# A hybrid decoder layer with 32 experts: x1 kept on chip, VectorE adds the ranks inside the last expert, and each next first weight quarter issued ahead of the down halves

## The reference

```
x1  = x + merge_branches(...)                  # residual, 520 rows
h   = rms_norm(x1, g_ffn)
logits = h @ w_router + b_router               # 32 experts
top_v, top_e = top_k(logits, 4); gates = softmax(top_v)
for each row and each of its 4 experts e:
    gu   = h @ w_gu[e] + b_gu[e]               # 1024 -> 2048
    gate = min(gu[:1024], 7); up = clip(gu[1024:], -7, 7)
    act  = (up + 1) * gate * sigmoid(1.702 * gate)
    y   += gates[e] * (act @ w_down[e] + b_down[e])
out = rms_norm(x1 + y, g_final)
```

## Time and profile before

| | |
|---|---|
| median of 3 runs | 1601.92 us (1600.48 to 1602.94) |
| the profiled execution's own time | 1602.56 us |
| its span, first to last instruction | 1600.6 us |
| mean granted TensorE clock | 0.982 |
| TensorE busy | 1542.3 us, 96% |
| VectorE busy | 797.2 us, 50% |
| ScalarE busy | 280.1 us, 18% |
| GpSimd busy | 211.1 us, 13% |
| moved by DMA | 514.10 MB, mean 321 GB/s |
| first gate/up matmul of the loop | at 537.77 us |
| last down matmul | ends at 1554.22 us |

### The profile page before, as it was taken

How to read it: one execution, slowest core, us unless ns; L and a number is a source line. 1 busy time by engine, 2 the same in 40 slices (tenths; PEclk the granted TensorE clock), 3 DMA queues, 4 the chain that set the end, 5 groups by cost and what they waited for, 6 DMA issues and landing times.

```text
span 1600.6 us, 32912 instructions
## 1 busy us (share of the span) xinstructions
PE 1542.3 (96%) x13183; PEld 711.9 (44%) x13183; DVE 797.2 (50%) x2035; ACT 280.1 (18%) x556; POOL 211.1 (13%) x278
## 2 busy tenths in 40 slices
PE   9999999999999899999999999999999999999982
PEld 7677487787745433333333333333333333333320
DVE  4349738605523553445444544544454445444538
ACT  2310020006211011112111111121112111211122
POOL 3634310015100000000000000000000000000015
PEclk9999999999999799999999999999999999999996
DMA  7455745713262599999999999999999999999984
GB/s 240 156 165 184 261 167 177 257 61 119 92 287 78 196 416 417 415 409 419 416 411 407 416 415 411 411 414 413 407 410 414 417 406 415 417 417 404 415 333 161
DMA packets 73820, 514.10 MB, mean 321 GB/s; under 512 B 13570, under 2 KB 14018, under 8 KB 48538
## 3 DMA queue, kind: packets, MB, share of 16 engines
q1 hardware_dynamic: 63378, 493.35, 77.3%
q0 software_dynamic: 10384, 20.01, 3.7%
HBM read 499.60 MB, written 22.37 MB: 326 GB/s over the span
## 4 chain that ended last, share of the span: by engine, by line
PE 70%; DMA 24%; DVE 2%; POOL 2%; issue 2%; ACT 1%; SPq 0%; DVEq 0%; POOLq 0%; ACTq 0%
PE PS L1322 34%; DMA weight_ring<-w_gu 22%; PE PS L938 16%; PE PS L1246 3%; PE PS L1328 3%; PE PS L989 2%; PE PS L1054 2%; PE PS L1334 2%; PE PS L1040 1%; PE PS L1104 1%; DMA region_x<-x_rows 1%; POOL region_x L716 1%; PE PS L1003 1%; POOL weight_ring L625 1%; PE PS L1279 1%
## 5 line engine op out<-in xcount | busy, mean ns | idle before, releaser
L1322 PE MATMUL PS<-weight_ring,region_experts 128*32 128x512 f32 x5376 | 597.6, 593 | 7.1 <-DMA weight_ring<-w_gu 5.9
L1322 PEld LDWEIGHTS PS<-weight_ring,region_experts 128*32 128x32 f32 x5376 | 169.9, 110 | 401.8 <-issue 365.3
L1740 DVE TENSOR_TENSOR region_experts<-PS,region_w 128x512 f32<-128x512 f32 x96 | 66.4, 692 | 464.2 <-PE PS L1322 464.2
L1328 PE MATMUL PS<-weight_ring,act_turned 128*32 128x512 f32 x2048 | 225.6, 592 | 0.0
L938 PE MATMUL PS<-region_x,region_w 128*128 128x260 f32 (+1 forms) x928 | 209.4, 385 | 1.0 <-DVE region_x L1545 1.0
L938 PEld LDWEIGHTS PS<-region_x,region_w 128*128 128x128 f32 x928 | 175.2, 190 | 33.1 <-issue 4.6
L1731 DVE STREAM_TRANSPOSE region_experts<-region_x 32x256 f32<-32x256 f32 x372 | 161.2, 433 | 4.7
L865 ACT ACTIVATE region_experts<-region_experts 128x256 f32<-128x256 f32 x96 | 40.0, 416 | 615.2 <-DVE region_experts L1742 615.2
L1328 PEld LDWEIGHTS PS<-weight_ring,act_turned 128*32 128x32 f32 x2048 | 66.5, 110 | 153.2 <-issue 153.2
L683 POOL DMA_INDIRECT y_k<-region_x,idx_y x31 | 29.0, 934 | 680.4 <-ACT region_x L889 658.5
L1334 PE MATMUL PS<-weight_ring,act_turned 128*32 128x256 f32 x2048 | 116.4, 379 | 0.0
(11 more groups left out here) (282 smaller groups left out, 1153.9 us busy)
## 6 DMA issues: line engine op xcount, KB each, us to landing
weight_ring<-w_gu SPq DMA_DIRECT2D x112, 2048.0 KB, 12.4
weight_ring<-w_down SPq DMA_DIRECT2D x64, 2048.0 KB, 13.7
ring_more<-w_gu SPq DMA_DIRECT2D x16, 2048.0 KB, 21.6
region_w<-w_mt SPq DMA_DIRECT2D x33, 512.0 KB, 4.2
weight_ring<-cache_kT SPq DMA_DIRECT2D x64, 256.0 KB, 4.1
weight_ring<-cache_v SPq DMA_DIRECT2D x64, 256.0 KB, 4.0
weight_ring<-w_out SPq DMA_DIRECT2D x2, 2048.0 KB, 9.9
weight_ring<-y_k SPq DMA_DIRECT2D x2, 2048.0 KB, 16.1
```

The lines of the kernel that those rows point to most:

```text
L1322: mm = pe.matmul(bank(g)[GRP * q:GRP * q + GRP], hTe[u][:, k, GRP * g:GRP * g + GRP], weights(k // 2, u)[:, k % 2, SEG * q:SEG * q + SEG], ...
L1328: mm = pe.matmul(bank(3)[GRP * j:GRP * j + GRP], actT[:, kk, GRP * g:GRP * g + GRP], w_dn[:, kk, 512 * h:512 * h + 512], start=(kk == 0), ...
L1740: dve.tensor_tensor(gu, bank(g), b_wide, ALU.add).then_inc(S["biased"], 1)
```

## The change

1. x1 stays in SBUF: a new region `x1_kept` holds its place, so `xn(t)` is not overwritten. `x1_rows` is gone, its store (except the 8 sample rows, `x1_tail`), its zero rows and its 2 MB load too. Several small tiles move (`gx`, `b_rows`, `iota_row`, `idx_f`, `idx_t`, `warm`, `ys`, `mq4`, `dnew`).
2. `yf` is now rank 0's place in the ring; the first addition is rank 0 plus `xn(t)`, so there are 16 additions of 128x1024, all on VectorE. The sample additions and the four of rank 0 stand inside the last expert, between its second and its third group.
3. GpSimd's last pair: zero scatter first, then expert 30's scatter, then `all_added`, then the unused gather.
4. SP: `ranks_load` issues rank 0 first, then the samples. The added samples are moved by one DMA instead of eight.
5. SP, in the loop: quarter 0 of expert e + 1 is issued behind quarter 3 of e, ahead of the down halves of e.
6. ScalarE: the Sqrt that loads the table (`warm`) moves behind the branch. Order of the tiles at the end: 4, 2, 3, 0, 1. The branch for further passes repeats the loads and additions with `again` = 1; it doesn't run.

```diff
-            def load(b, e, u, whole=True):
+            def load(b, e, u, ahead=True):
                 n = b * NE + e
-                if whole:
-                    gu_load(0, e, u)
                 sp.wait_ge(S["b_wide_done"], n)
                 bias_load(e)
                 for c in range(1, 3):
...
                 gu_load(3, e)
+                if ahead:
+                    gu_load(0, e + 1, 1 - u)
                 for c in range(2):
                     sp.wait_ge(S["down_done"], (n - 1) * 2 + c + 1)
                     down_load(c, e)
...
+            def ranks_load(again):
+
+                sp.wait_ge(S["all_added"], again + 1)
+                sp.dma_start(yk[0], rank_rows(0)).then_inc(S["y0_in"], 16)
+                for k in range(TOPE):
+                    sp.dma_start(ys[:, k, :], y_k[YROWS * k + 4 * P:YROWS * k + 4 * P + NS].rearrange("r (c x) -> (r c) x", x=64)).then_inc(S["ys_in"], 16)
+                sp.dma_start(ys[:, TOPE, :], x1_tail.rearrange("r (c x) -> (r c) x", x=64)).then_inc(S["ys_in"], 16)
...
-            sp.wait_ge(S["all_added"], 1)
-            sp.wait_ge(S["hTe_ready"], NE)
...
-            sp.dma_start(x1_all, x1_rows[0:4 * P].rearrange("(t p) x -> p t x", p=P)).then_inc(S["y0_in"], 16)
...
             def last_pair():
-                pair(0, NE // 2 - 1, True, True)
+
+                gather(0, NE - 1, 1)
+                po.wait_ge(scat[1], (NE // 2) * 16)
+                link(po, po.memset(ysc[1][0:CAP], 0.0), "po_step", n)
+                po.wait_ge(S["idx_kept"], NE)
+                scatter(NE - 1, 1, S["zeroed"])
+                po.wait_ge(S["y_ready"], NE)
+                scatter(NE - 2, 0, scat[0])
+                po.wait_ge(S["zeroed"], 16)
+                po.wait_ge(scat[0], (NE // 2 + 1) * 16)
+                po.memset(spare, 0.0).then_inc(S["all_added"], 1)
+                gather(0, NE, 0)
+                po.wait_ge(gath[0], (NE // 2 + 1) * 16)
...
                     group(ne, 1)
+                    if last and u == 1:
+                        add_samples(0)
+                        add_rank(0, 0)
                     group(ne, 2)
...
+            def add_samples(again):
+                dve.wait_ge(S["ys_in"], 16 * (TOPE + 1) * (again + 1))
+                for k in range(TOPE):
+                    if k:
+                        dve.wait_ge(S["ys_step"], TOPE * again + k)
+                    dve.tensor_tensor(ys[:, 0, :], ys[:, 0, :], ys[:, k + 1, :], ALU.add).then_inc(S["ys_step"], 1)
+
+            def add_rank(k, again):
+                if k == 0:
+                    dve.wait_ge(S["y0_in"], 16 * (again + 1))
+                elif k < 3:
+                    dve.wait_ge(yk_full[k - 1], 16 * (again + 1))
+                for m, t in enumerate(FIN_ORDER[1:]):
+                    if k == 3:
+                        dve.wait_ge(y3_full[t // 2], 16 * (again + 1))
+                    if k:
+                        dve.wait_ge(S["dve_sum"], SUMS * again + 4 * k - 3 + m)
+                    dve.tensor_tensor(yf[t], yf[t], yk[k][:, t, :] if k else xn(t), ALU.add).then_inc(S["dve_sum"], 1)
...
             def last_pair():
                 pair(0, NE // 2 - 1, True, True)
+                for k in range(1, TOPE):
+                    add_rank(k, 0)
```

More of the change, by code:

```diff
@@ L217, in build_step @@
         wo = [part(W6, slot(n), KD, 512) for n in range(2)]
+        mq4 = part(W6, slot(5) + 3600, P)[0:2]
+        dnew = part(W6, slot(5) + 3728, 2, 32)[0:32]
         def xn(t):
@@ L662, in gather, with scatter, pair @@
                     .then_inc(gath[u], 16)
-            def pair(b, i, first=False, last=False):
+            def scatter(e, u, signal):
+                po.indirect_dma_start(y_k, bass.IndirectOffsetOnAxis(ap=idx_y[u][0:CAP, :], axis=0),
+                                      ysc[u][0:CAP], None, bounds_check=Y_LAST, oob_is_err=False).then_inc(signal, 16)
+            def pair(b, i, first=False):
                 for u in range(2):
@@ L703, in _ @@
                         experts(b)
-            po.wait_ge(S["cnt_ready"], 1)
-            po.memset(spare, 0.0).then_inc(S["all_added"], 1)
-            po.wait_ge(S["y0_in"], 32)
-            for k in range(TOPE):
-                if 0 < k < 3:
-                    po.wait_ge(yk_full[k - 1], 16)
-                for t in (0, 1) if k < 3 else (0,):
-                    if k == 3:
-                        po.wait_ge(y3_full[t // 2], 16)
-                    if k:
-                        po.wait_ge(S["po_sum"], 2 * k - 1 + t)
-                    po.tensor_tensor(yf[t], yf[t], yk[k][:, t, :], ALU.add).then_inc(S["po_sum"], 1)
+                po.memset(spare, 0.0).then_inc(S["all_added"], 1)
         @block.scalar
@@ L908, in _ @@
                         experts(b)
+            act.activation(warm, eps_t, ACT.Sqrt)
             for n, t in enumerate(FIN_ORDER):
@@ L1809, in _ @@
                         experts(b)
+                add_samples(1)
+                for k in range(TOPE):
+                    add_rank(k, 1)
+                dve.wait_ge(S["ys_back"], 32)
             def fin_row(m):
```

119 lines of the change are left out of this document (45 added, 74 removed).

## The result

| | before | changed |
|---|---|---|
| median | 1601.85 us (1600.48 to 1602.94, 4 runs) | 1586.38 us (1585.86 to 1587.99, 4 runs) |
| profiled execution, its span | 1602.56, 1600.6 us | 1586.06, 1584.2 us |
| mean granted TensorE clock | 0.982 | 0.989 |
| TensorE, VectorE, GpSimd busy | 1542.3, 797.2, 211.1 us | 1539.9, 790.7, 187.3 us |
| moved by DMA | 514.10 MB | 509.52 MB |

The changed kernel takes 0.9906 of the time of before, 95% interval 0.9888 to 0.9923: 15.5 us less by the medians. 1586.7 was forecast. Four more runs on another chip gave 1585.77 (0.9901, 0.9886 to 0.9917). One execution in the whole study, of the kernel with x1 stored and loaded again, took 2144.99 us at a granted clock of 0.702; the ratios leave it out, but the median of that kernel counts it (1592.23, and 1591.06 without it).

What follows compares the result with a forecast made beforehand. TensorE and DMA were both near their limits in the loop, neither behind it. Start 0, loop 0, end 13.9 plus 1.3 made 15.2 us less: 1586.7 us against the median 1601.92, range 1579 to 1592.

Steps and rivals of the forecast that it cites:

- Start 0, loop 0: Before and in the expert loop: dropped stores and reordered weight loads were claimed to give 0 us each.
- the first rival (the loop gains): In the loop: the earlier first quarter brings the fourth in time, up to 12.1 us more gained, 1574.6; 12%.
- the third (down halves late): In the loop: down halves land too late and stop TensorE; 0.5 us costs 15.5, 1 us gives 1618; 5%.
- The flag: At the end: expert 30's scatter lands at 1534.1, so SP's loads start at 1534.5, 6.4 us earlier.
- Rank 0 and the samples: At the end: rank 0 lands 9.1 us after issue, at 1543.6; the samples 1.4 us later, at 1545.0.
- my best case: At the end: rank 0's load starts when the queue empties at 1536, takes 5.1 us, lands at 1541.1.
- 16 additions: On VectorE at the end: 1.21 us each without GpSimd; four for rank 0 take 4.8 us, twelve more 14.5.
- Third group and TensorE's stall: Third group, 3.0 us, ends at 1553.9; TensorE ends 3.3 us later, off the chain; falling clock adds 3.6 to L1334.
- VectorE's branch: On VectorE, now behind the additions: the branch over the further passes takes 0.47 us, ending at 1569.0.
- The second rival: At the end: rank 0 lands 4.7 us later or VectorE's branch costs 4.3 more; either gives 1591; 12%.
- First L1857 to the end: From the first final addition: 17.7 us before, 16.4 left, as the 1.28 us table load leaves the chain.
- the fourth rival: At the end: landing loads, not GpSimd, cause the 3.36 us additions; VectorE's 16 take 34 us more, 1621; 1%.

Runs made afterwards that it cites:

- the changed kernel again: The changed kernel unaltered, run once more on another chip as reference for follow-up kernels: 1585.77 us (0.9901), end 76.2.
- in halves: Changed kernel with rank 0 loaded in two halves, two tiles added ahead of the third group, the rest and samples behind: 1581.22 us (0.9873), again 1584.28 (0.9875).

## Why the prediction was right

By its own steps, times from SP's last expert issue (1508.60 before, 1508.10 changed):

- **Start 0, loop 0.** Right. The period was to stay within 0.1 us of 31.76 and was 31.82; the first rival (the loop gains) falls with the old weight order, and the third (down halves late) has no wait at L1330. The first quarter, now ahead of the down halves, lands 20.4 us after its issue. The second down half's landing is not in this trace, but it is in that of the changed kernel again, here for all experts and for the one whose load is issued at 1045.5:

```profile
DMA to landing us min/median/max: 14.7/22.2/22.9
```
```profile
DMA to landing us min/median/max: 22.3/22.3/22.3
```

  It lands at 1067.9. L1330 starts at 1066.67 there and needs this half 3.4 us later, so it is 2.2 us early, and 2.7 was forecast. The price that I had weighed is real, and it stayed hidden.
- **The flag.** 25.5 us forecast, 25.7 measured.
- **Rank 0 and the samples.** 36.4 forecast for the last sample, 37.6 measured, 1.2 late: rank 0 took 10.8 us and not 9.1. The step "I take the same: 9.1" was mis-sized; its bounds (to 13.8) held it. The reason is the last down half. In the trace of before it is issued at 1522.3 and lands 16.8 us later, at 1539.1, so the "queue empties at 1536" of my best case was 3 us too early. In the changed kernel again it is issued at 1522.4 and lands 17.8 us later, at 1540.2; rank 0, issued there at 1534.5, lands 10.8 us later, at 1545.3, which is that 1540.2 and its own 5.1 us.
- **16 additions.** 1.21 us each was right as a duration, but they overlap: from start to start it is 1.14 (4.54 us for four, 1546.62 to 1551.16). The 16 take 18.2 us instead of 19.4, which gives the 1.2 back.
- **Third group and TensorE's stall.** 3.0 and 3.3 forecast; 3.0 and 3.1. The clock fell, the case that I had only named, and L1336 took 1.7 us more; VectorE waits for nothing between its last rank addition and L1857, so that cost nothing.
- **VectorE's branch.** 0.47 forecast, nothing measurable: L1857 starts while the last addition ends. The second rival is out on both counts: rank 0 was 1.7 us slower and not 4.7.
- **First L1857 to the end.** 16.4 forecast, 16.45 measured.

Together 60.4 us to the first L1857 and 59.65 measured, an end of 76.8 forecast (92.0 less 15.2) and 76.1 measured. Two errors of 1.2 us cancelled, which is luck; the branch and 0.3 of small terms are the rest. That the median (1586.38) lies 0.3 us from the forecast is luck too, since the starts alone scatter by several us. The additions did become free (the fourth rival falls), by the mechanism named.

The 15.9 us can be laid out along the one chain, before and changed: from SP's last expert issue to the flag 32.1 and 25.7 us, from the flag to the first rank addition 16.9 and 12.9, from there to the first final addition 25.3 and 21.1 (with the third group in between), from there to the end 17.7 and 16.45. Each stretch gave something: 6.5, 4.0, 4.1 and 1.3.

The parts, each undone or done alone, tell why: additions on VectorE 5.8 us, x1 not loaded 5.1, flag ahead 3.3, table load 1.3 (by its own stretch; 0.8 by the end), together 15.5. No part gave nearly all, so the rival of one part falls. But my four parts leave out a fifth, which lost: the eight additions ahead of the third group, 1.2 us. With it the sum is 14.3, and 1.6 us remain that no run assigns, more than the 0.7 us by which an end repeats. Two parts were taken away from the changed kernel and two were added to the one before, so the sum need not close; what the loads' new order at the end and the single DMA for the samples gave was not tried alone. That the parts nearly add up is shown, that they add up exactly is not.

## What to carry to other kernels

Look at durations before counting engines: two engines that take 3.3 us each for what one does in 1.2 are slower together, and the one short instance in the trace says so. Where loads share a queue, the bytes ahead of the awaited one are its price, whole (2 MB, 5.1 us here), whereas an earlier issue is worth only what the queue does not take back (3.3 of 6.2 us). And once a wait for data is on the path, first fill it with work that needs no data (the third group: 1.2 us), then divide the load and do what needs only its first part (1.7 to 2.3 us more, for one more DMA).

## What the runs showed that I had not expected

- GpSimd's and VectorE's additions exclude each other almost wholly: 2.34 and 1.22 us alone, 3.3 to 3.4 each together.
- The 4.8 us in which TensorE stands still ahead of its final product, for which no release is recorded, shrink when the matmuls ahead get slow. From the start of the last 64 matmuls to the product it was 8.42 us before, 7.54 changed (matmuls at 1.2 GHz for part of the time) and 8.60 with the third group first. The first line below is of the changed kernel, the other two are of the one with the third group first:

```profile
PE PS L1409 <- issue: 2.2, 1, 2.2
```
```profile
1552.08 3.64 PE L1336 MATMUL PS<-weight_ring,act_turned 128*32 128x256 f32 x64
1560.68 1.86 PE L1409 MATMUL PS<-region_x 128*8 128x512 f32 x2 [4.97 <-issue]
```

  Over all kernels the stall is 4.3 to 5.0 us behind matmuls at full clock and 1.3 to 3.3 behind matmuls at 1.2 GHz, while the time from the start of the 64 matmuls to the product is 8.0 to 8.6 us with the former and 7.1 to 8.6 with the latter (in two of these five cases the profile names ScalarE's scaled copy as the release). So most likely the stall begins while the matmuls still run, and matmuls at 1.2 GHz cover more of it. The Trainium skill (Runtime: NRT & Kernel Launch, Instruction fetch mechanics) lets a taken branch outside the fetched pages wait for its target; that the stall is this fetch is argued, no run here took the branch away. On VectorE the same branch cost 0.47 us behind a 0.12 us instruction and nothing that can be seen behind 1.22 us additions.
- The start differs by up to 4.8 us over the kernels here, and by 3.5 us between two executions of one kernel (in halves: 554.3 and 557.8). I have no cause for it.
- The eight additions ahead of the third group, a part of the change, cost 1.2 us where they stand; all of its gain comes from the other parts.
